# A transformer block in split fp32: weights made stationary in 14 more blocks, and places of 4352 bytes in the weight rings

## The reference

```
h = rms_norm(x, pre_mix_norm);  proj = h @ w_in
(hq, hf, hi, hg, mq, mk, mv, dq, dkv, iq, ik, iw, gates) = split(proj)
y_a = hgrn2_mixer(hq, hf, hi, hg)          # f = lb + (1-lb)*sigmoid(hf), gated recurrence, 4 heads
y_b = moba_attention(mq, mk, mv)           # with 256 tokens: causal attention with a bias
y_c = dsa_attention(dq, rms_norm(dkv), iq, layer_norm(ik), iw)   # 64 best keys of an indexer
g = sigmoid(gates)                         # three gates of 1024 features per token
merged = g0*(y_a @ w_branch_a) + g1*(y_b @ w_branch_b) + g2*(y_c @ w_branch_c)
x = x + rms_norm(merged @ w_out, post_mix_norm)
gate, up = split(rms_norm(x, pre_ffn_norm) @ w_ffn_in)
x = x + rms_norm((silu(gate) * up) @ w_ffn_out, post_ffn_norm)
```

## Time and profile before

| | |
|---|---|
| median of 3 runs | 467.54 us (467.4 to 467.56) |
| the profiled execution's own time | 467.5 us |
| its span | 465.8 us |
| PE busy | 458.1 us, 98% |
| DVE busy | 301.6 us, 65% |
| ACT busy | 249.2 us, 54% |
| POOL busy | 49.0 us, 11% |
| granted TensorE clock, mean | 0.998 |
| DMA | 85.60 MB, mean 184 GB/s |

### The profile page before, as it was taken

One profiled execution on the slowest core, in us unless ns is written; L12 is line 12 of the kernel. 1 busy time (PEld: TensorE's weight loads), 2 busy tenths in 40 slices (PEclk: granted clock), 3 DMA queues, 4 the chain that ended last, 5 costly groups with the idle time before them and its releaser, 6 DMA issues.

```text
span 465.8 us, 8038 instructions
## 1 busy us (share of the span) xinstructions
PE 458.1 (98%) x3318; PEld 400.7 (86%) x3318; DVE 301.6 (65%) x403; ACT 249.2 (54%) x370; POOL 49.0 (11%) x50
## 2 busy tenths in 40 slices
PE   8999999999999999999999999999999999999994
PEld 7799798987788888888888888999999999888883
DVE  4657689898628746577449788766565665743532
ACT  5758369338485955526443462864544554443410
POOL 2301002456730100000000000100000000000000
PEclk9999999999999999999999999999999999999999
DMA  8997655545534454568565645666566566766202
GB/s 280 400 294 225 187 166 180 161 136 159 144 129 132 139 181 135 183 186 314 181 197 204 173 148 158 216 190 203 186 188 207 190 187 195 248 187 185 86 0 90
DMA packets 26025, 85.60 MB, mean 184 GB/s; under 512 B 3172, under 2 KB 4741, under 8 KB 25989
## 3 DMA queue, kind: packets, MB, share of 16 engines
q1 hardware_dynamic: 25268, 84.31, 56.1%
q10 hardware_dynamic: 720, 0.79, 0.5%
HBM read 83.84 MB, written 1.25 MB: 183 GB/s over the span
## 4 chain that ended last, share of the span: by engine, by line
PE 98%; DVE 1%; ACT 0%; issue 0%; DVEq 0%
PE bank L1450 56%; PE bank L1444 31%; PE bank L1476 2%; PE bank L1620 1%; PE bank L1485 1%; PE bank L1632 1%; PE bank L1660 1%; PE bank L1604 1%; PE bank L1509 1%; PE bank L1584 1%; PE bank L1575 1%; PE bank L1521 0%; PE bank L1526 0%; PE bank L1523 0%; PE bank L1633 0%; PE bank L1664 0%
## 5 line engine op out<-in xcount | busy, mean ns | idle before, releaser
L843 DVE TENSOR_TENSOR wl<-raw,wh 128x1024 fp32r<-128x1024 f32 (+1 forms) x150 | 185.0, 1268 | 45.9 <-ACT wh L514 45.7
L514 ACT ACTIVATE wh<-raw 128x1024 fp32r<-128x1024 f32 (+1 forms) x150 | 153.8, 1050 | 85.2 <-PE bank L1450 43.3
L1444 PE MATMUL bank<-hTh,wh 128*128 128x256 f32 x416 | 116.5, 280 | 0.0
L1444 PE MATMUL bank<-hTl,wh 128*128 128x256 f32 x416 | 115.4, 277 | 0.0
L1444 PE MATMUL bank<-hTh,wl 128*128 128x256 f32 x416 | 115.4, 277 | 0.0
L1450 PE MATMUL bank<-wh,hTh 128*128 128x512 f32 (+1 forms) x216 | 85.9, 398 | 0.2 <-DVE wl L843 0.2
L1450 PE MATMUL bank<-wh,hTl 128*128 128x512 f32 (+1 forms) x216 | 83.7, 388 | 0.0
L1450 PE MATMUL bank<-wl,hTh 128*128 128x512 f32 (+1 forms) x216 | 83.5, 387 | 0.0
L1444 PEld LDWEIGHTS bank<-hTh,wh 128*128 128x128 f32 x416 | 78.2, 188 | 0.5 <-issue 0.3
L1444 PEld LDWEIGHTS bank<-hTl,wh 128*128 128x128 f32 x416 | 78.3, 188 | 0.0
L1444 PEld LDWEIGHTS bank<-hTh,wl 128*128 128x128 f32 x416 | 78.1, 188 | 0.1
(11 more groups left out here) (227 smaller groups left out, 529.2 us busy)
## 6 DMA issues: line engine op xcount, KB each, us to landing
raw<-w_stream SPq DMA_DIRECT2D x146, 512.0 KB, 3.8
raw<-w_stream SPq DMA_DIRECT2D x4, 328.0 KB, 6.7
x<-x_in SPq DMA_DIRECT2D x4, 256.0 KB, 4.5
raw<-w_stream SPq DMA_DIRECT2D x4, 256.0 KB, 4.7
bias<-bias_scratch SPq DMA_DIRECT2D x8, 128.0 KB, 5.4
x<-x_in SPq DMA_DIRECT2D x1, 1024.0 KB, 5.7
out<-mo SPq DMA_DIRECT2D x3, 256.0 KB, 2.0
post<-post_mix ACTq DMA_DIRECT2D x1, 512.0 KB, 10.1
```

The lines of the kernel that those rows point to most:

```text
L514: did(act.activation(wh[:, u % SPLIT, place(u)], raw[:, u % RING, place(u)], ACT.Copy), high_done, u + 1 - EARLY)
L843: did(dve.tensor_tensor(wl[:, u % RING, place(u)], raw[:, u % RING, place(u)], wh[:, u % SPLIT, place(u)].bitcast(F32), ALU.subtract), low ...
L1444: ins = pe.matmul(bank[bk][:, i * S:(i + 1) * S], w_[:, k, h * P:(h + 1) * P], x_[:, kt, :], start=first, stop=final, skip_group_check=True)
```

## The change

The blocks hf and mk, the six gate blocks and the six branch blocks are computed by feature. Their transposes go, and so do those of merged, which is now kept features x tokens (merged2) and split straight from SBUF. The token norms are brought into a row (row1: a diagonal by VectorE, one TensorE job, one copy by ScalarE), and VectorE's new helper by_token multiplies the banks of hf, mk and the gates with it into SBUF, where ScalarE's sigmoids read them. TensorE's row1 product takes the ones that lie in qp. A place of the rings grows from 4224 to 4352 bytes, and the newly by-feature blocks start 16 floats into theirs.

```diff
@@ -64,9 +64,9 @@
 CHUNKS = DFF // 512
-BY_FEATURE = ("dq", "hq", "mq") + tuple(f"f{c}{j}" for c in "gu" for j in range(CHUNKS))
+BY_FEATURE = ("dq", "hf", "hq", "mq", "mk") + tuple(f"{n}{b}{c}" for n in ("gate", "branch") for b in BRANCHES for c in range(2)) + tuple(f"f{c}{j}" for c in "gu" for j in range(CHUNKS))
 SHIFTED = BY_FEATURE + ("uk",)
-SHIFT, PLACE = 16, 1024 + 32
+SHIFT, PLACE = 16, 1024 + 64
@@ -126,13 +126,13 @@
 N_MASKS = len(IN_STRIP) * HALF_STRIP
-JOBS = (["hT00", "hT10", "hT01", "hT11", "rel", "ckvT", "iqT0", "iqT1", "kc0", "kc1", "vc0", "vc1", "ikT"]
-        + [f"ix{i}" for i in range(6)] + ["hfT0", "hfT1",
+JOBS = (["hT00", "hT10", "hT01", "hT11", "rel", "ckvT", "iqT0", "iqT1", "row1", "kc0", "kc1", "vc0", "vc1", "ikT"]
+        + [f"ix{i}" for i in range(6)] + [
                                           "diag", "L1", "dl0", "dl1", "dl2", "L2", "L4", "L8", "L16",
-                                          "mkT0", "mkT1", "mkT2", "mkT3", "L32", "dP0", "dP1", "dP2", "dP3", "L64", "dO0", "dO1", "L128",
+                                          "L32", "dP0", "dP1", "dP2", "dP3", "L64", "dO0", "dO1", "L128",
                                           "ml0", "ml1", "ml2", "ho0", "ho1", "mP0", "mP1", "mP2", "mP3",
                                           "mO0", "mO1", "yaT0", "yaT1", "yaT2", "yaT3",
-                                          "mTa0", "mTa1", "mTa2", "mTa3", "mTb0", "mTb1", "mTb2", "mTb3", "h2T00", "h2T01", "h2T10", "h2T11",
+                                          "h2T00", "h2T01", "h2T10", "h2T11",
                                           "row", "fT"])
@@ -194,6 +194,7 @@
         sig = sb("sig", [P, 3, TT, 512])
+        row1 = sb("row1", [P, S])
         skip = [sb("skip0", [P, SHIFT])]
@@ -262,6 +263,9 @@
         row2 = row.rearrange("p (o s) -> p o s", o=1).to_broadcast([P, 2, S])
+        diag1 = prob[:, 0:S]
+        rows1 = row1[:].rearrange("p (o s) -> p o s", o=1).to_broadcast([P, 2, S])
+        merged2 = merged[:].rearrange("p t d -> p (t d)").rearrange("p (c t n) -> p c t n", c=2, t=TT)
@@ -288,7 +292,7 @@
             o_sums one_exp out_mean out_rstd out_squares out_sums prob_ready relu_used score_ready
-            silu_last silu_done row_diag fT_low fgu_high down_eps stored x1_ready x1_squares x_rstd x_squares y_high
+            silu_last silu_done row_diag row1_diag row1_ready gate_sig mT_low fT_low fgu_high down_eps stored x1_ready x1_squares x_rstd x_squares y_high
         """.split()
@@ -609,6 +613,8 @@
             copy_jobs(["iqT1"], lambda i: flat(iqT, 1))
+            ps = wait_job(act, "row1")
+            did(act.activation(row1[:], ps[:, 0:S], ACT.Copy), *job_read("row1"))
             high_until(17)
@@ -620,14 +626,11 @@
                 did(act.activation(relu[:, i % 2], ps[:, 0:512], ACT.Relu, scale=DI ** -0.5), *job_read(f"ix{i}"))
-            stage_copy("hf", 0, 512, 21)
-            high_until(22)
-
             high_until(24)
             for i in range(2):
-                ps = wait_job(act, f"hfT{i}")
-                did(act.activation(flat(pre, i), ps[:, 0:512], ACT.Sigmoid))
-                did(act.activation(flat(kT, i), ps[:, 0:512], ACT.Sigmoid, scale=-1.0), *job_read(f"hfT{i}"))
+                act.wait_ge(*block_read("hf", i))
+                did(act.activation(flat(pre, i), stage[:, 0, i], ACT.Sigmoid))
+                did(act.activation(flat(kT, i), stage[:, 0, i], ACT.Sigmoid, scale=-1.0))
             act.wait_ge(lb_ready, 1)
@@ -696,11 +699,6 @@
             normalise(0)
-            stage_copy("mk", 0, 512, LAST_UNIT["mk"] + 5)
-            high_until(40)
-            for r in range(NSTRIP):
-                ps = wait_job(act, f"mkT{r}")
-                did(act.activation(token_strip(kcT, r), strip_bank(ps), ACT.Copy), *job_read(f"mkT{r}"))
             high_until(41)
@@ -722,28 +720,29 @@
                 name = f"gate{b}{c}"
-                high_until(LAST_UNIT[name] + 4)
-                if c:
-                    after_block(act, f"branch{b}0")
+                high_until(LAST_UNIT[name] + 5)
                 for t in range(TT):
-                    ps = wait_block(act, name, t)
-                    did(act.activation(sig[:, b, t], ps[:, 0:512], ACT.Sigmoid, scale=stat(X_RS + t)), *block_read(name, t))
+                    act.wait_ge(*block_read(name, t))
+                    did(act.activation(sig[:, b, t], sig[:, b, t], ACT.Sigmoid), s["gate_sig"], TT * (3 * c + i) + t + 1)
...
             probT_copy("m")
-            gates(1, 0)
+            high_until(52)
             y_high(["mO0", "mO1"], 1, 1)
...
                 did(act.activation(token_strip(yh[0], r), strip_bank(ps), ACT.Copy), s["y_high"], 5 + r)
+            gates(1, 0)
             gates(2, 0)
             high_until(FIRST_UNIT[f"gate{BRANCHES[0]}1"] + 5)
+
             def m_high(c):
-                for r in range(NSTRIP):
-                    ps = wait_job(act, f"mT{'ab'[c]}{r}")
-                    did(act.activation(token_strip(mTh, r, 4 * c, 4), strip_bank(ps), ACT.Copy), s["mT_high"], 4 * c + r + 1)
+
+                for t in range(TT):
+                    act.wait_ge(s["merged"], 4 * c + TT + t + 1)
+                    did(act.activation(f_tiles(mTh, c, t), pair(merged2[:, c, t]), ACT.Copy), s["mT_high"], TT * c + t + 1)
@@ -921,6 +920,9 @@
                     s["ckv_ready"], t + 1)
+            for t in range(TT):
+                dve.wait_ge(eye_made, 1)
+                did(dve.tensor_scalar(diag1[:, t * P:(t + 1) * P], eye[:], stat(X_RS + t), None, ALU.mult), s["row1_diag"], t + 1)
             low_until(11)
@@ -977,7 +979,16 @@
+            def by_token(name, dst):
+
+                for t in range(TT):
+                    ps = wait_block(dve, name, t)
+                    did(dve.tensor_tensor(pair(dst(t)), pair(ps[:]), rows1, ALU.mult), *block_read(name, t))
+
             for i in range(6):
+                if i == 4:
+                    after_job(dve, "row1")
+                    by_token("hf", lambda t: stage[:, 0, t])
                 add_heads(i)
@@ -1083,6 +1094,7 @@
             low_until(37)
+            by_token("mk", lambda t: flat(kcT, t))
             level(4)
@@ -1127,7 +1139,15 @@
                         did(ins)
+            def gate_rows(i, c):
+
+                b = BRANCHES[i]
+                by_token(f"gate{b}{c}", lambda t: sig[:, b, t])
+
+            low_until(49)
+            gate_rows(0, 0)
             low_until(52)
+            gate_rows(1, 0)
             y_low(["mO0", "mO1"], 1, 1)
@@ -1141,17 +1161,17 @@
                     low_until(LAST_UNIT[f"branch{b}{c}"] + 3)
-                    after_block(dve, f"gate{b}{c}")
+                    dve.wait_ge(s["gate_sig"], TT * (3 * c + i + 1))
                     for t in range(TT):
                         ps = wait_block(dve, f"branch{b}{c}", t)
-                        dst = merged[:, t, c * 512:(c + 1) * 512]
+                        dst = merged2[:, c, t]
                         out_ = dst if i == 0 else tmp[:, t]
...
                         for t in range(TT):
-                            dst = merged[:, t, c * 512:(c + 1) * 512]
+                            dst = merged2[:, c, t]
                             n_merged[0] += 1
@@ -1165,15 +1185,18 @@
             def m_low(c):
-                for r in range(NSTRIP):
-                    ps = wait_job(dve, f"mT{'ab'[c]}{r}")
-                    dve.wait_ge(s["mT_high"], 4 * c + r + 1)
-                    did(dve.tensor_tensor(token_strip(mTl, r, 4 * c, 4), strip_bank(ps), token_strip(mTh, r, 4 * c, 4).bitcast(F32), ALU.subtract),
-                        *job_read(f"mT{'ab'[c]}{r}"))
-
+                for t in range(TT):
+                    dve.wait_ge(s["mT_high"], TT * c + t + 1)
+                    did(dve.tensor_tensor(f_tiles(mTl, c, t), pair(merged2[:, c, t]), f_tiles(mTh, c, t).bitcast(F32), ALU.subtract), s["mT_low"], TT * c + t + 1)
+
+            low_until(LAST_UNIT[f"gate{BRANCHES[2]}0"] + 4)
+            gate_rows(2, 0)
             merge(0)
...
             m_low(0)
+            for i in range(3):
+                low_until(LAST_UNIT[f"gate{BRANCHES[i]}1"] + 4)
+                gate_rows(i, 1)
             merge(1)
@@ -1438,9 +1461,9 @@
                             h = 2 * t + i
-                            for w_, x_ in ((rh, hTh), (rl, hTh), (rh, hTl)):
-                                first = kt == i == 0 and w_ is rh and x_ is hTh
-                                final = kt == n_kt - 1 and x_ is hTl
+                            for w_, x_ in ((rh, high), (rl, high), (rh, low)):
+                                first = kt == i == 0 and w_ is rh and x_ is high
+                                final = kt == n_kt - 1 and x_ is low
                                 ins = pe.matmul(bank[bk][:, i * S:(i + 1) * S], w_[:, k, h * P:(h + 1) * P], x_[:, kt, :], start=first, stop=final,
@@ -1560,6 +1583,9 @@
             transposes("iqT1", tiles(stage[:, 1], 0))
```

(21 more changed lines are left out.)

## The result

The changed kernel takes 465.0 us (median of 5 runs, 464.6 to 465.15) against 467.54 us for the kernel before in the same session (5 runs, 467.4 to 468.26): a ratio of 0.9941 with a 95% interval of 0.993 to 0.9953. It is faster by 2.5 us where 5.4 were forecast, and 465.0 lies above the range that was given. The profiled execution took 465.04 us, with a span of 463.3.

The account below looks back on a forecast made before the run. TensorE's own work was taken as the bound. Changed units -1.4, staying by-token -1.4, staying by-feature +0.5, transposes -3.5, row product +0.4 make -5.4 us from 467.5: 462.1 us, range 461.0 to 464.6.

Parts of the forecast that it names:

- Blocks turned to by feature: 44 units of hf, mk, gates and branches go to 2.73 us each on TensorE: -1.4 us.
- rival (d): Weight loads not hidden in the changed units, each then costing 3.03 us: slower, 475.2 us; chance 0.05.
- What bounds the kernel: TensorE, busy 98% of the span and 98% of the chain; time is the sum of what it executes.
- hf and mk: 8 of the 44 units turned to by feature; their share of the forecast change is -0.25 us.
- By-token units that stay: 25 odd by-token units each lose 0.055 us through the new places: -1.4 us; even ones unchanged.
- By-feature units that stay: 26 odd units already by feature (dq, hq, mq, fg, fu) go from 2.71 to 2.73 us: +0.5 us.
- Transposes and the row product: On TensorE, removed transposes with their edges save 3.5 us; the added fp32 product for token norms costs 0.4.
- Hidden work: VectorE's 16 added scalings, 11.1 us, and ScalarE's changed work stay behind TensorE; least margin 1.5 to 2 us, unit 33.
- (a): Layout misread: 462.5 us if it changes no pace, 465.1 if all by-token units are slow; chance 0.14.
- (b): VectorE late at unit 33 or behind it, TensorE waiting 1 to 2 us: 463.1 to 464.1 us; chance 0.08.
- (c): A fixed cost per matmul makes the 44 changed units 1.3 us dearer: 464.8 us; chance 0.03.
- What would show it: Profile signs: gate, branch and down units at 2.73 us, no TensorE wait; changed units above 2.76 mean (c) or (d).

Follow-up runs that it names:

- vector_double: The changed kernel with every VectorE scaling by the row of token norms done twice; 464.86 us, ratio 0.9923.
- kick_1: The changed kernel, all addresses kept, with one identity transpose put between weight units 53 and 54; 464.35 us in its one run.
- kick_4: The changed kernel, all addresses kept, with four identity transposes put between weight units 53 and 54; 463.45 us, ratio 0.9912.
- offset_192: The changed kernel with every by-feature weight starting 192 bytes into its place instead of 64; 466.68 us in a single run.
- wait_alone: The changed kernel with only a long-fulfilled wait on the bank's reader between units 53 and 54, no transpose; 465.11 us.

## Why the prediction was wrong

**The step that failed** is "Blocks turned to by feature", where 2.73 us a unit was taken because "the FFN's units are the same instructions in the same order". They are, and the pace still differed: the measured unit is 2.834, the 36 cost 102.51 us where the forecast has 99.2 (100.56 - 1.35), and this 3.3 us is more than the whole miss of 2.9. The assumption behind it was that the one by-feature pace in the earlier trace rows, read in the feed-forward part, is the only one. The trace of before held the other pace. This piece of its chain is three by-feature units, 18 to 20:

```profile
59.97 8.58 PE bank L1444 x72
```

8.58 us, where three times 2.72 would make 8.16 (units 18 and 19 go at the slow pace, 20 at the fast one); and in its timeline the matmuls of unit 19 stand 0.12 apart in the middle of the unit, far from any edge:

```profile
63.77 0.28 PE L1444 MATMUL bank<-hTl,wh 128*128 128x256 f32 x1
63.89 0.28 PE L1444 MATMUL bank<-hTh,wh 128*128 128x256 f32 x1
64.01 0.28 PE L1444 MATMUL bank<-hTh,wl 128*128 128x256 f32 x1
64.13 0.28 PE L1444 MATMUL bank<-hTl,wh 128*128 128x256 f32 x1
```

The prediction passes over these and over the single pieces of 2.82 and 2.83 us. The bound that I kept for this unknown, 3.03 a unit, went into rival (d) as an all-or-nothing case; the value between, a second steady pace, was no case at all.

Point by point:
- **What bounds the kernel** was right: TensorE's own work, no wait of it that isn't at the very start.
- **hf and mk**: forecast -0.25, measured -0.03, the same cause: units 14, 15 and 30 went at 117.8 ns.
- **By-token units that stay**: the right mechanism, and its size a little too small: -2.13 against -1.80 (-1.4 for the pace, -0.4 for two interludes). I let the even units stay at 2.735 us; they gained too, and all down units now settle at 2.72. The one term that "no row of before can prove" held.
- **By-feature units that stay**: +0.30 forecast (+0.5 for the pace, -0.2 for an interlude), +0.11 measured. Their long piece is 97.94 us in both kernels; the 2.73 that I took for even places was no effect of the place.
- **Transposes and the row product**: -2.3 forecast, -2.33 measured. The product is the row of 0.43 us at 36.86, where the forecast has it.
- **Hidden work** was right, and vector_double shows that 8.5 us more of VectorE would still be hidden.
- **Rivals.** (a) gives 465.1 for "all by-token units slow" (465.0 with the 28 even units that the plan has, where the prediction counts 30). That is the measured time, by luck: the mechanism isn't there, the by-token units are all fast. (b) did not happen. (c), a fixed cost per matmul, gives 464.8 and is refuted by its own test: at the fast pace two matmuls of 256 columns take 2 x 113.3 = 226.6 ns and one of 512 takes 226.7. At the slow pace they take 235.6, so a gap is there or not with one and the same instruction. By the Trainium skill's rule ("TensorE: Matmul & The Clock Gate", "Back-to-back issue gap"), which the page gives for the isolated gap, the pair should cost 2.5 ns more always; the runs show 0 or 9. (d) is excluded at its own place (3.03 a unit), though its direction was the true one; 2.834 is close under its break-even of 2.853, which is why the change still wins.
- **What would show it**: "changed units above 2.76" did name the failure before the result, and 2.83 is what the profile has.

The form and the layout are not additive: -4.0 and -4.1 us alone, -2.5 together. The old places let by-feature stretches return to the fast pace and make the odd by-token units slow; the equal places free the by-token ones, and leave the by-feature gates in whichever pace they enter. Different starts by use (by-token at equal places, by-feature at 64 and 192 in turn) give both.

## What to carry to other kernels

Before one pace is put into a sum, divide every long piece of the chain by its count, everywhere in the trace; where the same instruction has two quotients, there are two states, and a moved block can land in either. Try a change of form and a change of layout apart from each other: here each was worth more alone than both together. And when addresses differ from unit to unit in a pattern such as 16.5 x 256 bytes, ask what the difference does for each kind of access before it is evened out.

## What the runs showed of the hardware

- A weights-stationary fp32r matmul of 256 columns runs back to back at 113.3 or 117.8 ns at a granted clock of 1.00, with the stationary tile 64 or 192 bytes past a multiple of 256; with 32, 128 and 0 bytes, in one execution each, the long pieces ran at 118.3, 118.7 and 120.0 and no unit at 113.3. Bytes are counted from the ring's start; where the rings begin isn't on record.
- The pace is kept over 36 units (864 matmuls, 97.94 us) and changed by one foreign transpose of 128 columns, in either direction (at each of the 4 that two kernels put in; in kick_1 the fast steps begin five matmuls behind it). Four transposes changed it in kick_4 and, between units 93 and 94, in the changed kernel, but not there in offset_192; the row's product of two fp32 passes between units 91 and 92 left it slow. A wait that is already fulfilled changes nothing.
- With places of 4352 bytes the by-token matmul of 512 columns takes 226.7 ns in every place; with 4224 bytes and the 128-byte step between neighbours, the 22 down units take 60.84 in place of 59.88 us.
- The pace of a short stretch can differ between executions: wait_alone and the changed kernel are one program up to unit 53, and unit 30 took 113.3 ns a matmul in the one and 117.8 in the other. The long stretches agreed in these two, and the changed kernel's five times (464.6 to 465.15) leave no room for a switch of the gates, worth 2.6 to 3.9 us.
- What makes the two paces isn't settled. The records of the weight loads give no sign of it: in the changed kernel all but a few start 2 to 5 ns behind the start of a matmul in the slow stretch (200 to 230 us) and 3 to 4 ns in the fast one (330 to 380 us), and last 187 to 192 and 187 to 188 ns. It isn't the granted clock, 1.00 in both windows. What decides which foreign work changes the pace wasn't tried on purpose: other widths, other counts and other places of the operand are open.
